# Rotary halves exchanged by transfers within SBUF in place of TensorE products, in a two-block transformer kernel on one core

## The chip, the cores and the metric

The kernel runs on one NeuronCore of one Trainium2 chip. The metric is the device time of one execution in microseconds (us), and of several executions the median. Engines are named as in the profile: PE is TensorE (PEld its weight loads), DVE is VectorE, ACT is ScalarE, POOL is GpSimd, SP is SyncE. A name with a q (ACTq, SPq) is that engine's queue where it issues a DMA.

## What is computed

Two transformer blocks run one after the other on 512 tokens of width 1024 (the second on 528, with 16 meta tokens in front). Only the first block's attention input matters here. The normalised input is projected to latent queries and keys and to the queries and keys of a dilated attention. Each head is normalised, and four kinds of head tile are then rotated by position:

```python
def rope(x, positions):
    d = x.shape[-1]
    half = d // 2
    inv_freq = jnp.power(ROPE_THETA, -2.0 * jnp.arange(half) / d)
    ang = positions[:, :, None, None] * inv_freq
    cos, sin = jnp.cos(ang), jnp.sin(ang)
    x1, x2 = x[..., :half], x[..., half:]
    return jnp.concatenate([x1 * cos - x2 * sin, x1 * sin + x2 * cos], axis=-1)
...
qd = rope(rms_norm(qd, g_dil_q), positions)          # 8 heads of 64
kd = rope(rms_norm(kd, g_dil_k), positions)          # 8 heads of 64
q_pe = rope(rms_norm(q[..., 64:], g_mla_q_pe), positions)   # 8 heads of 32
k_pe = rope(rms_norm(k_pe, g_mla_k_pe), positions)          # one of 32, shared by the heads
```

So each element needs itself times a cosine, plus its partner half a head away times a sine, with a minus sign in the first half. The attentions, the output projection, the two feed-forward stages and the second block (a state-space mixer and a gated recurrent mixer) follow and are not touched.

## The kernel before

Activations lie transposed: features on the 128 partitions, 512 tokens along the free axis. Weights come in units of 128 x 1024 float32 (512 KB) through two stage buffers, loaded by SP. ACT rounds each unit to a high part (`split_hi`, L906, instruction L912), and DVE forms the low part (`split_lo`, L2148, instruction L2151). PE multiplies three times per 128 x 128 block, high by high, high by low and low by high (`products`, L1458, instruction L1467). There are four slots of high and low parts, so ACT splits a unit only when the job that used its slot has ended (L911), and SP loads a stage buffer only when DVE has finished the unit in it (`stage_free`, L694).

Each engine's instructions stand in one order written out by hand, and semaphores join them. `Plan` only counts units and jobs. `ahead(name, j)` on ACT and on DVE (L993, L2333) splits the unit four ahead of the one that job `name, j` has just made free.

The stage around the change runs the jobs ql, kvl, dq (4 tiles), dk (4), qp (2), kpe (1), kn (4), qn01 (2) and qn23 (2), then the values mv and dv. A job is one tile of 128 features, 24 products for ql to dk and kpe, 12 for qp and qn, 6 for kn. Jobs alternate between two accumulators, so job n waits until ACT has read job n-2. ACT's `raw` (L1028) reads a finished job twice, once squared into `sqg` (L1043) and once times its gain into the tile's place in `HT` (L1048). The head tiles form five groups (`GROUPS`, L568): group 0 is dq, 1 is dk, 2 is qp and kpe, 3 is kn, 4 is qn. The first three are rotated, in six pieces (`ROTS`, L616): two pieces of two tiles for each group, but for the last, (2,1), which is the kpe tile alone.

For a group the four engines work as follows.

- PE's `group_stats` (L1673, L1682) sums the squares of a head with a block matrix of ones, once the squares are there, into PSUM banks 4 to 7.
- ACT's `group_log` (L1058, L1062) and `group_exp` (L1065, L1068) make the inverse root, each behind a load of its function table.
- PE's `group_rot` (L1685, instruction L1695) multiplies each tile of a piece by a signed permutation matrix `r64` or `r32` of the constants and so puts the partner half, with its sign, into PSUM banks 1 and 3. It waits for the tiles from ACT and for DVE to have read the banks for the piece before.
- POOL's `cosines` (L2992, L2997) multiplies the tiles in place in `HT` by the cosines, when PE's products are done.
- DVE's `rotated` (L2338) multiplies PSUM by the sines into `rtp` (L2345), waits for POOL, and adds `rtp` to `HT` (L2349). DVE's `scaled` (L2351, L2356) multiplies a whole group by the inverse roots and signals `ghead_done`.

`sqg` is two buffers that groups take in turn. So ACT's first `raw` of group g waits for `scaled` of group g-2 (L1042): kn 0 waits for group 1, and qn01 0 for group 2.

The tables of cosines and sines are made by DVE (`table`, L2202) from the positions and the inverse frequencies in the constants `misc`, and ACT takes the sine of all four at L1085.

The order on ACT from there is: raw dk 0, raw dk 1, group_log(0), raw dk 2, group_exp(0), raw dk 3, raw qp 0, ahead kpe, group_log(1), raw qp 1, group_exp(1), raw kpe, raw kn 0, raw kn 1, group_log(2), raw kn 2, group_exp(2), raw kn 3, raw qn01 0, group_log(3), and so on (L1086 to L1109). The order on DVE is at L2388 to L2415, that on PE at L1720 to L1745, and that on POOL at L3013 to L3021.

Transfers that ACT issues before are loads of parameters at the start (L976), stores of spilled tiles (L1260) and, in the state-space part, moves within SBUF (L1283). SP moves rows of `HT` within SBUF ahead of the second attention (L786 to L794).

## Time and profile before

| | us |
|---|---|
| median of 3 runs | 1760.17 |
| lowest and highest | 1756.51, 1763.28 |
| the profiled execution, its own time | 1757.67 |
| its span, first to last instruction | 1755.9 |
| PE busy in it | 1696.6 (97%) |

The profile shows one execution. Its span is 1.8 us shorter than the time of the same execution. Rows give starts in us from the span's start, then lengths in us, unless marked as nanoseconds. A matmul of float32 operands is recorded as two passes, so 11 products of PE stand as 22 in a row. A bracket at the end of a row gives the idle time of that engine ahead of the instruction and the instruction that ended it.

### The profile page before, as it was taken

Reading aid. Unit: us, or ns where it says so; the run is one execution under the profiler, and the core shown is the slowest. Engines: PE = TensorE matmul, PEld = TensorE weight load, DVE = VectorE, ACT = ScalarE, POOL = GpSimd, SP = SyncE. Lnnn points to the kernel's source line nnn. Section 1 sums busy time; section 2 is a strip of 40 time slices with the busy share of each in tenths; the row PEclk is TensorE's granted clock in tenths of the full one; section 3 lists DMA queues with packets and bytes.
Section 4 is the critical chain, followed back from the end, with each engine's and each line's share of the span. In section 5 each row is a group of like instructions: output and inputs, shape, how many; then the busy total and the mean of one; then the engine's idle time right before and its main releaser. Section 6 shows DMA issues by size and latency. Waiting matters only on the chain.

```text
span 1755.9 us, 32153 instructions
## 1 busy us (share of the span) xinstructions
PE 1696.6 (97%) x12653; PEld 1507.2 (86%) x12653; DVE 1091.8 (62%) x1748; ACT 744.7 (42%) x1111; POOL 298.1 (17%) x286
## 2 busy tenths in 40 slices
PE   5999999999999999899999999999999999999998
PEld 4776766788888888799999999999999899989986
DVE  6756577677664578855868663343753766654633
ACT  4367574465332342632323544346233643322323
POOL 2112196311000002532005221110102000000002
PEclk8999999999999999999999999999999999999999
DMA  9354532433333232263435752332543233332332
GB/s 311 110 145 106 157 109 74 143 89 104 96 96 108 84 98 73 80 180 119 131 104 159 218 138 86 97 109 81 167 120 97 65 92 96 89 102 84 96 94 75
DMA packets 321167, 201.17 MB, mean 115 GB/s; under 512 B 51280, under 2 KB 303815, under 8 KB 320919
## 3 DMA queue, kind: packets, MB, share of 16 engines
q1 hardware_dynamic: 300976, 160.79, 32.2%
q0 software_dynamic: 7952, 24.83, 4.7%
q10 hardware_dynamic: 12118, 13.88, 2.3%
q8 instruction: 84, 1.38, 0.3%
q14 instruction: 37, 0.30, 0.0%
HBM read 177.75 MB, written 17.24 MB: 111 GB/s over the span
## 4 chain that ended last, share of the span: by engine, by line
PE 82%; DVE 7%; ACT 4%; issue 2%; SPq 2%; DMA 1%; POOL 1%; ACTq 0%; DVEq 0%; POOLq 0%
PE ps L1467 68%; SPq L854 2%; DVE wlo L2151 1%; PE ps L1768 1%; PE ps L1667 1%; PE ps L1778 1%; PE ps L1794 1%; PE ps L1608 1%; PE ps L1998 1%; PE ps L1682 1%; DVE acol L2226 1%; PE ps L2094 1%; PE ps L1584 1%; ACT whi L912 1%; PE ps L2090 1%
## 5 line engine op out<-in xcount | busy, mean ns | idle before, releaser
L1467 PE MATMUL ps<-zhi,whi 128*128 128x258 f32 (+2 forms) x2072 | 638.5, 308 | 3.4 <-DVE wlo L2151 1.4
L1467 PE MATMUL ps<-zlo,whi 128*128 128x258 f32 (+2 forms) x2072 | 633.5, 306 | 0.0
L1467 PE MATMUL ps<-zhi,wlo 128*128 128x258 f32 (+2 forms) x2072 | 632.1, 305 | 0.0
L1467 PEld LDWEIGHTS ps<-zhi,whi 128*128 128x128 f32 x2072 | 390.9, 189 | 28.1 <-issue 3.0
L2151 DVE TENSOR_TENSOR wlo<-stage,whi 128x1024 fp32r<-128x1024 f32 x256 | 322.5, 1261 | 139.0 <-ACT whi L912 127.1
L1467 PEld LDWEIGHTS ps<-zlo,whi 128*128 128x128 f32 x2072 | 390.2, 188 | 19.3 <-issue 1.0
L1467 PEld LDWEIGHTS ps<-zhi,wlo 128*128 128x128 f32 x2072 | 390.9, 189 | 18.2
L912 ACT ACTIVATE whi<-stage 128x1024 fp32r<-128x1024 f32 x256 | 269.3, 1054 | 315.8 <-PE ps L1467 260.2
L1467 PE MATMUL ps<-ghi,whi 128*128 128x512 f32 x340 | 134.7, 396 | 0.0
L1467 PE MATMUL ps<-glo,whi 128*128 128x512 f32 x340 | 134.2, 395 | 0.0
L1467 PE MATMUL ps<-ghi,wlo 128*128 128x512 f32 x340 | 134.0, 394 | 0.0
L1201 ACT ACTIVATE ub<-ps 128x512 f32<-128x512 f32 (+1 forms) x88 | 52.6, 597 | 162.7 <-PE ps L1467 161.4
L3034 POOL TENSOR_TENSOR zu<-zu,sq 128x528 f32<-128x528 f32 (+1 forms) x18 | 31.7, 1760 | 425.5 <-ACT sq L920 424.6
L2564 DVE TENSOR_SCALAR cv<-ub,par 128x512 f32<-128x512 f32 (+1 forms) x88 | 49.0, 557 | 70.2 <-ACT ub L1201 70.2
L1211 ACT ACTIVATE ghi<-cv 128x512 f32 (+1 forms) x44 | 27.9, 634 | 124.5 <-DVE cv L2579 124.5
L1467 PEld LDWEIGHTS ps<-ghi,wlo 128*128 128x128 f32 x340 | 64.0, 188 | 15.0
L1467 PEld LDWEIGHTS ps<-ghi,whi 128*128 128x128 f32 x340 | 63.9, 188 | 14.7
L1467 PEld LDWEIGHTS ps<-glo,whi 128*128 128x128 f32 x340 | 63.9, 188 | 14.6
L3027 POOL TENSOR_SCALAR pb<-pb,small 128x128 f32<-128x128 f32 (+3 forms) x64 | 72.8, 1155 | 9.9 <-DVE small L2454 9.5
L2573 DVE SCALAR_TENSOR_TENSOR cv<-ub,par,cv 128x512 f32<-128x512 f32 (+1 forms) x88 | 66.3, 754 | 13.1 <-DVE cv L2567 6.7
L2480 DVE TENSOR_TENSOR xT<-ps,xT 128x512 f32 (+2 forms) x30 | 20.8, 692 | 85.1 <-PE ps L1467 85.1
L1258 ACT ACTIVATE spill<-ps 128x516 f32<-128x516 f32 (+1 forms) x40 | 24.1, 604 | 103.1 <-PE ps L1467 103.0
(426 smaller groups left out, 2854.4 us busy)
## 6 DMA issues: line engine op xcount, KB each, us to landing
stage<-in_w_up_dram SPq DMA_DIRECT2D x88, 512.0 KB, 3.8
stage<-in_w_in_dram SPq DMA_DIRECT2D x74, 512.0 KB, 4.0
stage<-in_w_down_dram SPq DMA_DIRECT2D x32, 512.0 KB, 3.9
ring<-in_w_ada_dram POOLq DMA_DIRECT2D x24, 512.0 KB, 4.6
adab<-in_w_ada_dram SPq DMA_DIRECT2D x16, 512.0 KB, 8.2
stage<-in_w_down_dram SPq DMA_DIRECT2D x16, 384.0 KB, 3.4
stage<-in_w_o_dram SPq DMA_DIRECT2D x8, 512.0 KB, 4.0
ring<-in_w_ada_dram SPq DMA_DIRECT2D x8, 512.0 KB, 3.8
```

The source lines that it names most:

```text
L854: sp.dma_start(y5[SH * g:SH * g + SH, k, :].rearrange("p (j c) -> p j c", j=LC), y_view[g])\
L912: act.activation(whi[u % NHL][:], stage[slot][:], ACT.Copy).then_inc(hi_done, 1)
L1201: act.activation(wide(ub[:, j % 2, 2:2 + T], T), acc(job, T), ACT.Copy).then_inc(emptied[job % 2], 1)
L1211: act.activation(ghi[c % 2][:, bass.ds(i * 2 + q, 1), 0:T].rearrange("p a t -> p (a t)"), cv[:, q, 1, 0:T], ACT.Copy).then_inc(ghi_done, 1)
L1258: act.activation(wide(spill[m % 2][:, T2 - T:T2], T), acc(n, T), fn).then_inc(emptied[n % 2], 1)
L1467: last = pe.matmul(out, w(a, k), x(k, t0, t1), start=(k == 0 and a is whi and x is x_hi), stop=(k == ks - 1 and a is wlo))
L2151: dve.tensor_tensor(wlo[u % NHL][:], stage[plan.w_load[u] % NST][:], whi[u % NHL][:].bitcast(F32), ALU.subtract).then_inc(split_done, 1)
L2480: ins = dve.tensor_tensor(x, acc(job, T), x, ALU.add)
L2564: link(dve.tensor_scalar(o, ub[:, g, 2:2 + T], tap(2), par[:, bass.ds(i * 2 + (ROW[f["cb"]] + ft), 1)], ALU.mult, ALU.add))
L2573: dve.scalar_tensor_tensor(out=o, in0=ub[:, g, 0:T], scalar=tap(0), in1=o, op0=ALU.mult, op1=ALU.add).then_inc(conv_done, 1)
L3027: pool.tensor_scalar(pb[:, t % 4, r, 0:w], pb[:, t % 4, r, 0:w], total(t, r, 32), None, ALU.mult)\
L3034: pool.tensor_tensor(square(n, 0), square(n, 0), square(n, 1 + j % 2), ALU.add).then_inc(acc_done, 1)
```

## The change

PE's products with the signed permutation are gone, with `rot` and the two matrices in the constants. ACT issues transfers from `HT` to `rtp` that exchange the halves, 4 for a piece of heads of 64 (each of 32 partitions) and 8 for a piece of heads of 32 (each of 16 partitions), 32 in all. The minus sign goes into the frequencies: those of the first half are negative, which leaves the cosine as it was and turns the sine's sign. DVE's product with the sines reads `rtp` in place of PSUM and is one instruction for two tiles. `gsin_done` is now signalled by DVE's final addition, so a piece's transfers, which write `rtp`, wait for the addition of the piece before.

```diff
@@ host_constants
-    misc[:, 0], misc[:, 1] = inv64, inv32
+    misc[:, 0], misc[:, 1] = np.where(p % 64 < 32, -inv64, inv64), np.where(p % 32 < 16, -inv32, inv32)
...
-    return np.concatenate([ident, ones, misc, b64, b32, rot(64), rot(32)] + mla + dil + [chunk],
+    return np.concatenate([ident, ones, misc, b64, b32] + mla + dil + [chunk],
...
+        TURN_DMAS = [P // (GROUPS[g]["w"] // 2) for g, _ in ROTS]
+        TURNS_IN = [16 * sum(TURN_DMAS[:i + 1]) for i in range(len(ROTS))]
+        JOB_OF = {t: job for job, (t, g, _) in RAW.items() if g >= 0}
@@ ACT
+            def half_turn(g, p):
+
+                t0, n, _ = piece(g, p)
+                i, h = ROTS.index((g, p)), GROUPS[g]["w"] // 2
+                for t in range(t0, t0 + n):
+                    wait_job_out(act, JOB_OF[t])
+                if i:
+                    act.wait_ge(gsin_done, i)
+                for r in range(0, P, 2 * h):
+                    for d, f in ((r, r + h), (r + h, r)):
+                        act.dma_start(rtp[d:d + h, 0:n, :], HT[f:f + h, t0:t0 + n, :]).then_inc(grot_in, 16)
...
             act.activation(tab[:, :, :], tab[:, :, :], ACT.Sin).then_inc(tab_done, 1)
+            half_turn(0, 0)
             raw("dk", 0)
             raw("dk", 1)
+            half_turn(0, 1)
             group_log(0)
             raw("dk", 2)
             group_exp(0)
             raw("dk", 3)
+            half_turn(1, 0)
             raw("qp", 0)
             ahead("kpe", 0)
             group_log(1)
+            half_turn(1, 1)
             raw("qp", 1)
             group_exp(1)
+            half_turn(2, 0)
             raw("kpe", 0, False)
             raw("kn", 0)
             raw("kn", 1)
+            half_turn(2, 1)
             group_log(2)
             raw("kn", 2)
             group_exp(2)
@@ PE
-            def group_rot(g, p):
-                t0, n, _ = piece(g, p)
...
-                for m in range(n):
-                    mm = pe.matmul(ps[:, 1 + 2 * m, :], const("r%d" % GROUPS[g]["w"]), HT[:, t0 + m, :], start=True, stop=True)
-                mm.then_inc(grot_mm, 1)
...
-            group_rot(0, 0)
...
-            group_rot(2, 1)
@@ DVE, rotated
-                dve.wait_ge(grot_mm, i + 1)
+                dve.wait_ge(grot_in, TURNS_IN[i])
                 dve.wait_ge(tab_done, 1)
-                for m in range(n):
-                    ins = dve.tensor_tensor(rtp[:, m, :], ps[:, 1 + 2 * m, :], tab[:, w + 1, :], ALU.mult)
-                ins.then_inc(gsin_done, 1)
+                link(dve.tensor_tensor(rtp[:, 0:n, :], rtp[:, 0:n, :], tab[:, w + 1:w + 2, :].to_broadcast([P, n, T1]),
+                                       ALU.mult))
+                dve.wait_ge(gcos_done, i + 1)
+                dve.tensor_tensor(HT[:, t0:t0 + n, :], HT[:, t0:t0 + n, :], rtp[:, 0:n, :], ALU.add).then_inc(gsin_done, 1)
                 dve.wait_ge(gsin_done, i + 1)
-                dve.wait_ge(gcos_done, i + 1)
-                link(dve.tensor_tensor(HT[:, t0:t0 + n, :], HT[:, t0:t0 + n, :], rtp[:, 0:n, :], ALU.add))
@@ POOL, cosines
-                pool.wait_ge(grot_mm, ROTS.index((g, p)) + 1)
+                pool.wait_ge(grot_in, TURNS_IN[ROTS.index((g, p))])
```

## Rows read from the trace of the kernel before

**Rows 1.** The page: engines' busy time, and shares of the chain that ended last

```profile
PE 1696.6 (97%) x12653; PEld 1507.2 (86%) x12653; DVE 1091.8 (62%) x1748; ACT 744.7 (42%) x1111; POOL 298.1 (17%) x286
PE 82%; DVE 7%; ACT 4%; issue 2%; SPq 2%; DMA 1%; POOL 1%; ACTq 0%; DVEq 0%; POOLq 0%
```

**Rows 2.** The chain that ended last, 60 to 230 us: start, length, what

```profile
112.43 1.72 PE ps L1695 x4
...
143.97 2.81 PE ps L1467 x12
...
153.58 1.92 ACT sqg L1068
...
163.68 1.10 PE ps L1695 x2
...
168.95 3.43 PE ps L1682 x8
172.39 2.79 PE ps L1467 x12
```

**Rows 3.** The line of PE's products with the permutation: ns min/median/max

```profile
L1695 PE MATMUL ps<-HT,cst x22: 590/592/667, 112.3 to 164.2; 128*128 128x512 f32 x22
```

**Rows 4.** Timeline of ACT, 130 to 164 us: start, length, line, operation

```profile
130.52 0.60 ACT L1043 ACTIVATE sqg<-ps 128x512 f32<-128x512 f32 x1 [4.39 <-PE ps L1467]
...
147.94 1.28 ACT L1062 ACT_TABLE_LOAD   x1
149.23 1.98 ACT L1062 ACTIVATE sqg<-ps,small 128x2048 f32<-128x2048 f32 x1
151.11 0.58 ACT L1043 ACTIVATE sqg<-ps 128x512 f32<-128x512 f32 x1
...
156.45 1.06 ACT L912 ACTIVATE whi<-stage 128x1024 fp32r<-128x1024 f32 x1
...
161.54 1.54 ACT L1062 ACTIVATE sqg<-ps,small 128x1536 f32<-128x1536 f32 x1
```

**Rows 5.** Loads of the qn weights by SP, 131 to 143 us: issues; KB each, landing

```profile
130.92 11.44 SPq L703 DMA_DIRECT2D stage<-in_w_q_b_dram  x14
stage<-in_w_q_b_dram SPq DMA_DIRECT2D x14, 64.0 KB, 2.1
```

**Rows 6.** Lines of the rotation on POOL and DVE: duration ns min/median/max

```profile
L2997 POOL TENSOR_TENSOR HT<-HT,tab x6: 1296/2484/2956, 114.8 to 164.9; 128x1024 f32<-128x1024 f32 x5, 128x512 f32<-128x512 f32 x1
L2349 DVE TENSOR_TENSOR HT<-HT,rtp x6: 693/1226/1226, 117.4 to 166.3; 128x1024 f32<-128x1024 f32 x5, 128x512 f32<-128x512 f32 x1
```

**Rows 7.** A DVE line with two SBUF inputs, alone and beside POOL's product

```profile
L2324 DVE SCALAR_TENSOR_TENSOR asum<-ring,csil,asum x14: 1277/1282/3391, 98.3 to 208.8; 128x1024 f32<-128x1024 f32 x14
157.24 2.88 POOL L2997 TENSOR_TENSOR HT<-HT,tab 128x1024 f32<-128x1024 f32 x1 [5.71 <-PE ps L1695]
157.81 3.39 DVE L2324 SCALAR_TENSOR_TENSOR asum<-ring,csil,asum 128x1024 f32<-128x1024 f32 x1
```

**Rows 8.** Issues and landings of transfers by line, ns and us

```profile
L1283 ACTq DMA_DIRECT2D TT<-K x32: 592/646/1497, 882.3 to 974.8; - x32
DMA to landing us min/median/max: 2.1/3.2/4.8
L791 SPq DMA_DIRECT2D HT<-HT x2: 603/656/708, 220.3 to 221.7; - x2
HT<-HT SPq DMA_DIRECT2D x2, 128.0 KB, 2.4
887.70 0.33 ACTq L1260 DMA_DIRECT2D f_scratch<-spill  x1
888.13 1.06 ACT L912 ACTIVATE whi<-stage 128x1024 fp32r<-128x1024 f32 x1 [0.46 <-ACT spill L1258]
```

**Rows 9.** Busy time and granted clock (PEclk) by stretch, us

```profile
15.60:25.85 10.25, 6.81 (x53) 5.61 (x52) 9.82 (x19) 6.19 (x10) 0.00 (x0) 0.98 0.94 278
25.85:36.10 10.25, 7.21 (x22) 5.82 (x23) 8.94 (x17) 3.64 (x6) 0.00 (x0) 0.52 1.02 337
```

More of the change, by code:

```diff
@@ L72, in host_constants @@
     b32 = (p[:, None] // 32 == p[None] // 32) * 1.0
-    def rot(w):
-        r = np.zeros((P, P))
-        for m in range(P):
-            j = m % w
-            if j < w // 2:
-                r[m + w // 2, m] = -1.0
-            else:
-                r[m - w // 2, m] = 1.0
-        return r
     qi, ki = p[:, None], p[None]
@@ L101, in host_constants @@
     misc[:, 64:] = p[:, None] // 16 == 2 * (p[None, :64] // 16)
-    return np.concatenate([ident, ones, misc, b64, b32, rot(64), rot(32)] + mla + dil + [chunk],
+    return np.concatenate([ident, ones, misc, b64, b32] + mla + dil + [chunk],
                           axis=1).astype(np.float32)
-CONST = {n: i * P for i, n in enumerate(["ident", "ones", "misc", "b64", "b32", "r64", "r32", "mla", "_m1",
+CONST = {n: i * P for i, n in enumerate(["ident", "ones", "misc", "b64", "b32", "mla", "_m1",
                                          "_m2", "_m3", "dil", "_d1", "_d2", "_d3", "chunk"])}
@@ L419, in emit @@
         lat_sum = sem("lat_sum")
-        grot_mm, gcos_done, gsin_done, ghead_done = (sem("grot_mm"), sem("gcos_done"),
+        grot_in, gcos_done, gsin_done, ghead_done = (sem("grot_in"), sem("gcos_done"),
                                                               sem("gsin_done"), sem("ghead_done"))
@@ L1683, in group_stats @@
                 mm.then_inc(gstat_mm, 1)
-            def group_rot(g, p):
-                t0, n, _ = piece(g, p)
-                last = [J["dq"] + 3, J["dk"] + 3, J["qp"] + 1][g] if (g, p) != (2, 1) else J["kpe"]
-                wait_job_out(pe, last)
-                wait_job_out(pe, last - 1)
-                if g == 0 and p == 0:
-                    pe.wait_ge(s_cst2, 16)
-                if (g, p) != (0, 0):
-                    pe.wait_ge(gsin_done, ROTS.index((g, p)))
-                for m in range(n):
-                    mm = pe.matmul(ps[:, 1 + 2 * m, :], const("r%d" % GROUPS[g]["w"]), HT[:, t0 + m, :], start=True, stop=True)
-                mm.then_inc(grot_mm, 1)
             lat = (zx(lhi), zx(llo))
@@ L1720, in _ @@
             z1("dk", 0)
-            group_rot(0, 0)
             z1("dk", 1)
             group_stats(0)
-            group_rot(0, 1)
             z1("dk", 2)
@@ L1728, in _ @@
             several("qp", 0, 4, lat)
-            group_rot(1, 0)
             group_stats(1)
             several("qp", 1, 4, lat)
-            group_rot(1, 1)
             z1("kpe", 0)
             several("kn", 0, 2, kvl)
-            group_rot(2, 0)
             several("kn", 1, 2, kvl)
```

## The prediction

> **What bounds the kernel now.** I read the page first: PE is busy 97% of the span and holds 82% of the chain that ended last [rows 1]. By that alone, any PE time removed would come off the total. The share is an average, so I then read the chain through the stage of the change, 104 to 215 us. The reader is to see three parts in it [rows 2]. Up to 146.8 us it is PE's products without a gap, the permutation among them. From the end of qp 1 (143.97 + 2.81 = 146.78) it lies on ACT and DVE: the split of a unit, group 1's logarithm and exponential, then `scaled`, one sum of DVE, a split and a product, until PE's last permutation product starts at 163.68 [rows 2, 7]. Then PE again, until qn01 1 ends at 172.39 + 2.79 = 175.18. So in the last third of the rotations ACT has no room [rows 4]: from 147.94 to 166 its rows follow each other almost without a gap.
>
> From 175.18 on, ACT, PE and DVE hand on to each other with no part of the change among them. I take it that a shift of that moment goes through to the end, since everything behind is bound by PE in order. So the question is where the end of qn01 1 goes.
>
> **What is removed.** 22 recorded passes of 0.59 us, overlapping [rows 3]: a pair of products takes 1.72 us of the chain, the single one 0.86 (half of it; its row reads 1.10, behind an idle of PE) [rows 2]. That is 5 x 1.72 + 0.86 = 9.5 us. Three pairs lie ahead of the end of qp 1, where PE bounds: 5.2 us come off, and qp 1 ends at 141.6. The other 4.3 us lie where ACT bounds, and count only as far as ACT lets them. PE's wait for the banks goes too, and two blocks of constants fewer are loaded; nobody waits for them, so nothing.
>
> **What is added on ACT.** 32 issues. An issue holds the queue: the store at 887.70 takes 0.33, and the next ACTIVATE starts at 888.13 [rows 8]. For a transfer within SBUF no row has exactly this shape. Nearest are ACT's own, 0.646 us at the median, and SP's of rows of the same tile, 0.603 and 0.708; a store to HBM at 0.33 is the low end, and 0.9, between the median and the longest row of 1.5, the high end for a mean over eight. I take 0.65: 2.6 us for a piece of four, 5.2 for one of eight, 4 x 2.6 + 2 x 5.2 = 20.8 us in all. From the last issue to landing I take 2.4, the 128 KB of the same tile; bounds 2.1 and 4.8 [rows 8].
>
> The Trainium skill, "DMA: Bandwidth & Descriptors", section on issuing engines not being separate DMA queues, says that the sequencer time of an issue is usually small beside the transfer. Taken at its word it would make this the second case below, not the sum: four issues at 2.6 us are no smaller than a landing of 2.4.
>
> **What is added on DVE and POOL.** The product with the sines becomes one instruction of 128 x 1024 with two SBUF inputs, 1.22 us like the addition [rows 6], where before it were two from PSUM. It is released together with POOL's cosines (2.4 us) by the same semaphore. Side by side they don't overlap: a DVE line of two SBUF inputs that takes 1.28 us alone took 3.39 when it started 0.57 us into POOL's product, and ended 1.08 after it (157.81 + 3.39 against 157.24 + 2.88) [rows 7]. So from landing to the end of the addition a piece takes 2.4 + 1.15 + 1.22 = 4.8 us; without the collision it would be 3.7.
>
> **Waits added.** ACT waits in `half_turn` for DVE's addition of the piece before, and behind that wait stand its raws, which free PE's accumulators. That is how the delay reaches PE.
>
> **The sum, walked in order.** The first three pieces are covered. (0,0) is issued at 111.5 to 114.1, its addition ends by 121; (0,1) is issued 121.6 to 124.2 and done by 130.9; (1,0) is issued 134.8 to 137.4, done by 145.2. ACT waited 4.39 us for PE in that stretch [rows 4], and raw dk 2, exp 0 and raw dk 3 still come about 2 us earlier than before. If that cover were gone, these three would cost up to 7.8 us more. SP's loads of qn23 hang on DVE's split of kn, behind `scaled` 0: its last issue was at 142.4 [rows 5], becomes about 140.2, and lands 2.1 later. ACT's split of qn23 therefore starts at about 142.4, not 146.9. POOL's ring loads keep their places.
>
> From there, with the lengths of [rows 4] (split 1.05, raw 1.1, logarithm of four 3.25 with its table, of three 2.8, exponential 3.2 [rows 2] and 2.8):
> - split to 143.4, log 1 to 146.65, issues of (1,1) to 149.25, raw qp 1 to 150.3, exp 1 to 153.5 (before: 155.5, still 2 ahead);
> - (1,1) lands at 151.0, addition done at 155.85. ACT stands 2.4 us before it may issue (2,0): 155.9 to 161.1, landing at 162.85;
> - raw kpe, split, raw kn 0, raw kn 1 to 165.4. DVE's split of the mv unit starts into POOL's cosines and ends at 166.4, then product and addition to 168.8. ACT stands 3.4 us, issues (2,1) to 174.0;
> - log 2 to 176.8, raw kn 2 to 177.9, exp 2 to 180.7, raw kn 3 to 181.8;
> - PE: sums of group 3 from 181.3 (3.43), qn01 1 to 187.55.
>
> Against 175.18 that is **+12.4 us**. In terms: 9.5 us of PE gained, of which 4.5 still stand at ACT's split, against 13.0 of issues behind it ((1,1), (2,0), (2,1)), 5.8 of waiting for DVE, less 1.9 of waits of before that are swallowed: -4.5 + 13.0 + 5.8 - 1.9 = 12.4. With both low ends (0.33 and 2.1) the same walk gives 180.9, +5.7; with both high ends (0.9 is then cut to 0.9 x 8 = 7.2 an octet, landing 4.8) 195.5, +20.3.
>
> The profiled execution took 1757.67 (span 1755.9 and 1.8 around it), 2.5 below the median of 1760.17; runs spread from 1756.5 to 1763.3. The shift is added to the median: 1772.6.
>
> **The rivals.**
> - *Issues cost nearly nothing, or overlap ACT's work.* With none at all, landing and collision as above, the walk gives qn01 1 at 176.9: +1.7, or 1762. It decides below about 0.2 us an issue. Against it: rows of ACT's queue at 0.65, with nothing beside them. For it: the store at 0.33, and that each new transfer has few, long rows. I put here everything between +1 and +6.
> - *Faster: PE's time comes off.* If besides cheap issues POOL and DVE did not collide, the waits for `gsin_done` shrink, and the walk gives 172.2: -3; with all 9.5 us realised, -9.5, or 1750.7. It needs issues under 0.1 us and landings that ACT never waits for. PE's 97% speaks for it; the ACT rows from 147 us speak against.
> - *PE's clock falls.* In my walk PE works only about 11 us of the 30 between 151.7 and 181. A stretch in which it was busy 6.8 of 10.25 us was followed by one at a clock of 0.52, half of 2.4 GHz [rows 9]. At half speed qn01 0 would end at 183.5, the sums of group 3 at 190.4 and qn01 1 at 196.0, 8.5 later: +20.9, or 1781. Against it: at half speed the work ahead would fill PE and might bring the clock back in time.
> - *The change doesn't do what it says.* The diff leaves no permutation product, so the PE time must go; the cosine is even, the sine odd. No chance of its own.
>
> **How the numbers follow.** 0.5% is 8.8 us, about what a measurement of this kernel tells from no change. The forecast, +7 to +18, has 0.52, of which 0.05 is below 8.8; the fallen clock 0.17; cheap issues 0.24; faster 0.07, of which 0.04 is beyond 0.5%. So slower 0.47 + 0.17 = 0.64, same 0.05 + 0.24 + 0.03 = 0.32, faster 0.04. The range runs from +1 (1761) to +24 (1784): it leaves out the faster case, 0.07, a fringe of cheap issues below +1, 0.06, and what a fallen clock together with long landings would give beyond, 0.06.
>
> **What the profile after would show.** Right: no L1695; ACTq rows of 0.6 us in fours and eights, ACT's next row only behind them; an idle of 2 to 4 us of ACT ahead of (2,0) and (2,1), ended by DVE's addition; that sine product at well over 1.22 us, or POOL's cosines at over 2.4, in most pieces; qn 1 of qn01 ending near 187.5; PE with gaps of some 10 us between 150 and 180. Wrong: ACT's ACTIVATEs running beside the issues, issues near 0.3, landings under 2, or qn01 1 ending before 175.2. Wrong in size: a granted clock of a half in 160 to 190, or issues over 0.8 while SP is issuing too. If qn01 1 ends 12 us late and the total is not longer, then the assumption that the shift goes through was the error.

## The result and the profile after

The changed kernel takes **1780.1 us** (median of 4 runs, 1777.1 to 1781.9) against 1760.0 beside it: ratio **1.0117 (95% interval 1.0103 to 1.0130)**, slower by 20.1 us. The forecast was 1772.6, slower, with a range of 1761 to 1784. So the sign and the range held, and the sum of +12.4 was 7.7 us short. Where those are is the main question below.

The profiled execution has a span of 1777.3, against 1755.9. Two moments cut that difference of 21.4 into three parts. The first is the start of ACT's sine of the tables, just ahead of the first product of the rotation (L1085 before, L1090 after). The second is the start of `raw` qn01 1, from where on the prediction let the shift go through.

| | before | after | difference |
|---|---|---|---|
| start to sine | 109.63 | 111.79 | +2.2 |
| **stage**: sine to raw qn01 1 | 65.57 | 80.53 | +15.0 |
| **rear**: raw qn01 1 to the end | 1580.7 | 1585.0 | +4.3 |

The profiles are single executions. That of the kernel before took 1757.7, 2.5 below the median of 1760.2; that of the changed kernel took 1779.2, 0.9 below its median. If start and stage grew in every execution as in these two, the medians leave 20.1 - 2.2 - 15.0 = 2.9 us for the rear (an estimate), not 4.3.

First the page's busy time and shares of the chain, which answer to [rows 1].

```profile
PE 1697.6 (96%) x12631; PEld 1510.9 (85%) x12631; DVE 1095.6 (62%) x1743; ACT 744.8 (42%) x1111; POOL 298.7 (17%) x286
PE 79%; DVE 6%; ACT 4%; issue 3%; SPq 2%; DMA 2%; POOL 2%; ACTq 1%; DVEq 0%; POOLq 0%
```

PE made 22 passes fewer and was still busy 1.0 us longer, since part of its work ran at a lower clock (last view of this section). Its share of the chain went from 82% to 79%.

The timeline of ACT, 147 to 178 us, answers to [rows 4]: start, length, engine, line, operation, and in brackets the idle time ahead and what ended it. L1053 is the new transfer, L1036 and L1041 are `raw`.

```profile
147.51 1.06 ACT L905 ACTIVATE whi<-stage 128x1024 fp32r<-128x1024 f32 x1 [2.39 <-DMA stage<-in_w_q_b_dram]
148.18 0.51 ACTq L1053 DMA_DIRECT2D rtp<-HT  x1
148.59 1.28 ACT L1067 ACT_TABLE_LOAD   x1
148.72 1.26 ACTq L1053 DMA_DIRECT2D rtp<-HT  x2
149.89 1.97 ACT L1067 ACTIVATE sqg<-ps,small 128x2048 f32<-128x2048 f32 x1
150.01 0.61 ACTq L1053 DMA_DIRECT2D rtp<-HT  x1
...
154.23 1.91 ACT L1073 ACTIVATE sqg<-sqg 128x2048 f32<-128x2048 f32 x1
159.50 5.00 ACTq L1053 DMA_DIRECT2D rtp<-HT  x8
164.55 0.60 ACT L1036 ACTIVATE sqg<-ps 128x512 f32<-128x512 f32 x1 [8.41 <-issue]
...
168.81 0.60 ACT L1036 ACTIVATE sqg<-ps 128x512 f32<-128x512 f32 x1 [1.07 <-PE ps L1478]
169.30 0.68 ACT L1041 ACTIVATE HT<-ps,par 128x512 f32<-128x512 f32 x1
172.45 5.00 ACTq L1053 DMA_DIRECT2D rtp<-HT  x8
177.48 1.28 ACT L1067 ACT_TABLE_LOAD   x1 [7.50 <-issue]
```

The four issues of (1,1) stand beside a split, a table load and the logarithm, and cost ACT nothing. The octets of (2,0) and (2,1) stand alone: ACT idles 8.41 and 7.50 us, of which 5.0 each are issues, the rest (3.4 and 2.5) a wait for the piece before. These two idles, 15.9 us, are about as long as the whole growth of the stage, 15.0.

What ACT waits for is in the timelines of DVE and POOL (L2336 product with the sines, L2339 addition, L2347 `scaled`, L2143 split, L2988 cosines). They answer to [rows 6, 7].

```profile
130.66 1.22 DVE L2336 TENSOR_TENSOR rtp<-rtp,tab 128x1024 f32<-128x1024 f32 x1 [5.80 <-DMA rtp<-HT]
134.25 1.23 DVE L2339 TENSOR_TENSOR HT<-HT,rtp 128x1024 f32<-128x1024 f32 x1 [2.37 <-POOL HT L2988]
135.51 1.23 DVE L2143 TENSOR_TENSOR wlo<-stage,whi 128x1024 fp32r<-128x1024 f32 x1
...
154.65 1.23 DVE L2336 TENSOR_TENSOR rtp<-rtp,tab 128x1024 f32<-128x1024 f32 x1 [4.74 <-DMA rtp<-HT]
158.17 1.22 DVE L2339 TENSOR_TENSOR HT<-HT,rtp 128x1024 f32<-128x1024 f32 x1 [2.30 <-POOL HT L2988]
```

```profile
118.62 2.53 POOL L2988 TENSOR_TENSOR HT<-HT,tab 128x1024 f32<-128x1024 f32 x1
130.70 3.44 POOL L2988 TENSOR_TENSOR HT<-HT,tab 128x1024 f32<-128x1024 f32 x1 [9.55 <-DMA rtp<-HT]
154.69 3.38 POOL L2988 TENSOR_TENSOR HT<-HT,tab 128x1024 f32<-128x1024 f32 x1 [10.11 <-DMA rtp<-HT]
```

The last issue of (1,1) starts at 150.01 and its data land 4.6 us later, where DVE takes them up at 154.65, not 2.4. Then DVE's product (start 154.65) and POOL's (154.69) collide. DVE is 0.04 us ahead and takes its usual 1.23; POOL takes 3.38, and the addition waits 2.30 for it. (2,0) is issued when that addition ends. The Trainium skill, "SBUF — State Buffer", section on who interferes with whom, says that a DVE instruction with two SBUF inputs contends with a GpSimd instruction that reads SBUF, that the ports they share are an exclusive lock, and that the order of issue decides who blocks. The trace agrees in both directions: where POOL was ahead, at 118.62, DVE's product took 3.40.

Last PE's busy time and granted clock by stretch; they answer to [rows 9]. A row has the stretch and its length, the busy time and number of instructions of PE, PEld, DVE, ACT and POOL, then the granted clock as a share of 2.4 GHz, the DMA share and GB/s.

```profile
147.00:154.00 7.00, 5.00 (x22) 3.80 (x21) 2.30 (x2) 6.44 (x6) 0.00 (x0) 1.00 0.94 226
154.00:160.00 6.00, 1.07 (x4) 0.31 (x2) 3.02 (x3) 2.13 (x2) 3.38 (x1) 0.51 0.00 0
160.00:171.00 11.00, 5.13 (x9) 3.18 (x10) 7.18 (x5) 4.36 (x7) 2.37 (x1) 0.50 0.32 51
171.00:182.00 11.00, 4.88 (x17) 3.19 (x16) 3.57 (x3) 4.49 (x5) 1.80 (x2) 0.81 0.30 79
182.00:188.00 6.00, 6.00 (x17) 3.97 (x16) 3.35 (x3) 5.63 (x8) 0.00 (x0) 0.76 0.18 70
```

PE was busy 1.07 us of the 6 from 154 on, and from there to 171 it got half of 2.4 GHz. It idled again (6.12 us ahead of 181.53) and the clock was 0.76 on average in the last stretch, where its work stands on the chain.

### The profile page after: what moved, and what is told of

Read it like the earlier page. It is cut to its first block, busy times and chain, and to the rows that moved or that the text cites. A ratio compares the mean times of both kernels' runs of the same rounds, so it can differ in the third digit from the quotient of the medians.

```text
span 1777.3 us, 32136 instructions
## 1 busy us (share of the span) xinstructions
PE 1697.6 (96%) x12631; PEld 1510.9 (85%) x12631; DVE 1095.6 (62%) x1743; ACT 744.8 (42%) x1111; POOL 298.7 (17%) x286
## 4 chain that ended last, share of the span: by engine, by line
PE 79%; DVE 6%; ACT 4%; issue 3%; SPq 2%; DMA 2%; POOL 2%; ACTq 1%; DVEq 0%; POOLq 0%
PE ps L1478 65%; SPq L847 2%; PE ps L1595 1%; DVE wlo L2143 1%; PE ps L1619 1%; PE ps L1760 1%; PE ps L1678 1%; PE ps L1770 1%; PE ps L1786 1%; PE ps L1990 1%; ACT whi L905 1%; PE ps L2086 1%; POOL HT L2988 1%; DMA xrow<-in_x_dram 1%; PE ps L2082 1%
## 5 line engine op out<-in xcount | busy, mean ns | idle before, releaser
L2143 DVE TENSOR_TENSOR wlo<-stage,whi 128x1024 fp32r<-128x1024 f32 x256 | 325.2, 1272 | 139.8 <-ACT whi L905 127.7
L3025 POOL TENSOR_TENSOR zu<-zu,sq 128x528 f32<-128x528 f32 (+1 forms) x18 | 31.6, 1757 | 425.6 <-ACT sq L913 424.7
L3018 POOL TENSOR_SCALAR pb<-pb,small 128x128 f32<-128x128 f32 (+3 forms) x64 | 72.7, 1154 | 9.6 <-DVE small L2445 9.2
```

Of the source, the lines that this page charges most:

```text
L2143: dve.tensor_tensor(wlo[u % NHL][:], stage[plan.w_load[u] % NST][:], whi[u % NHL][:].bitcast(F32), ALU.subtract).then_inc(split_done, 1)
L3018: pool.tensor_scalar(pb[:, t % 4, r, 0:w], pb[:, t % 4, r, 0:w], total(t, r, 32), None, ALU.mult)\
L3025: pool.tensor_tensor(square(n, 0), square(n, 0), square(n, 1 + j % 2), ALU.add).then_inc(acc_done, 1)
```

## The experiments

Stage and rear are cut as above. Medians are of the runs named by the experiment, ratios against the kernel before on the same chip, with 95% intervals.

| | what | us | ratio | stage | rear |
|---|---|---|---|---|---|
| before | | 1760.2 | | 65.6 | 1580.7 |
| after | | 1780.1 | 1.0117 (1.0103 to 1.0130) | 80.5 | 1585.0 |
| e1 | after, again | 1779.2, one run | | 80.6 | 1585.0 |
| e2 | two buffers | 1767.9 | 1.0047 (1.0033 to 1.0061) | 69.4 | 1587.7 |
| e3 | one transfer a piece | 1764.3 | 1.0022 (1.0010 to 1.0033) | 66.5 | 1587.2 |
| e4 | cosines apart | 1768.3 | 1.0051 (1.0035 to 1.0066) | 72.8 | 1582.3 |
| e5 | before, products cut | 1755.7 | 0.9977 (0.9968 to 0.9987) | 61.7 | 1579.9 |
| e6 | POOL issues | 1788.9 | 1.0163 (1.0149 to 1.0177) | 86.4 | 1588.4 |
| e7 | e2 and e4 | 1765.7 | 1.0035 (1.0022 to 1.0049) | 68.7 | 1582.7 |
| e8 | three pieces by PE | 1759.2 | 1.0000 (0.9990 to 1.0011) | 65.1 | 1580.0 |
| e9 | before, +17.2 on PE | 1777.6 | 1.0101 (1.0087 to 1.0116) | 82.7 | 1580.8 |
| e10 | before, +6.9 on PE | 1767.3 | 1.0044 (1.0031 to 1.0057) | 72.7 | 1581.8 |
| e11 | e8, splits first | 1765.4 | 1.0031 (1.0019 to 1.0043) | 69.9 | 1585.3 |
| e12 | e8 without a stall | 1759.0 | 0.9989 (0.9979 to 0.9999) | 62.4 | 1584.7 |

### e1: the changed kernel a second time

> The changed kernel as it is, for a second profile. In its first profile the end of qn01 1 came 17.1 us later than before (192.3 against 175.2), of which 2.0 us were there at 95 us, ahead of every part of the change, and the end came 21.4 us later, 4.3 us more, with three short stretches of half clock behind 320 us that the profile before doesn't have. Theory: the rotary stage itself costs 15 us, and the 2.0 and the 4.3 belong to the execution; a second profile then shows another split of them, with the stage (from the sine at L1090 to the end of qn01 1, 80.5 us in the first) within 1.5 us of the first. Rival: they belong to the change, and come back at the same places within 0.3 us.

Stage 80.6, rear 1585.0, each within 0.1 us of the first profile, and the sine starts at 111.79 again. The rival held: the parts repeat. But both executions took 1779.2 us, so they say little about the slower ones, up to 1781.9, and nothing about the kernel before.

### e2: two buffers for the swapped halves

```diff
-        rtp = at("rtp", [P, 2, T1], TAB + 8192 + 4096)
+        rtp = [at("rtp0", [P, 2, T1], TAB + 8192 + 4096), at("rtp1", [P, 2, T1], SQO)]
...
-                if i:
-                    act.wait_ge(gsin_done, i)
+                if i > 1:
+                    act.wait_ge(gsin_done, i - 1)
...
```

> Transfers go to two buffers in turn, so ACT waits for DVE's addition of the piece before the last, not of the last. Theory, that ACT stands for DVE's addition ahead of both pieces of eight (3.4 us and 2.5 us in the profile, and the issues could start earlier still, beside the exponential): 8 us less than the changed kernel, a ratio of about 1.007 to the kernel before, and raw kpe some 6 us earlier. Rival, that what costs is the time of the eight issues alone (5.0 us twice): at most 2 us less, ratio 1.010 or more. Rival, the fallen clock: no change of the ratio beyond 0.001.

The total fell by 12 us and the stage by 11.2, more than the 8 expected. ACT's timeline shows why one wait is worth more than its own length:

```profile
149.10 1.28 ACT L1074 ACT_TABLE_LOAD   x1
149.16 1.80 ACTq L1054 DMA_DIRECT2D rtp<-HT  x3
150.39 1.91 ACT L1074 ACTIVATE sqg<-sqg 128x2048 f32<-128x2048 f32 x1
150.98 3.17 ACTq L1054 DMA_DIRECT2D rtp<-HT  x5
154.20 0.60 ACT L1037 ACTIVATE sqg<-ps 128x512 f32<-128x512 f32 x1 [1.89 <-issue]
```

Without the wait, (2,0)'s octet runs beside the table load and the exponential, so ACT idles 1.89 us where it idled 8.41. The wait was not only 3.35 us long: it also parted the issues from the work that hid them.

### e3: one transfer for a piece

```diff
-                for r in range(0, P, 2 * h):
-                    for d, f in ((r, r + h), (r + h, r)):
-                        act.dma_start(rtp[d:d + h, 0:n, :], HT[f:f + h, t0:t0 + n, :]).then_inc(grot_in, 16)
+                act.dma_start(rtp[:, 0:n, :], HT[:, t0:t0 + n, :]).then_inc(grot_in, 16)
```

> One transfer of 128 partitions in place of the 4 or 8 of a piece: the same bytes and waits, 6 issues in place of 32. It leaves out the exchange of the halves. Theory of issues on the path: the pieces of eight hold ACT 0.4 us instead of 5.0; half of that is given back, since the bytes of a piece land about 4.8 us behind one issue where they landed 2.2 behind the last of eight: about 6 us less than the changed kernel, ratio 1.008. Rival, the bytes and their landing are the cost: no more than 2 us less, ratio 1.010 or more. If all 9.2 us come off, landing was off the path, ratio 1.006.

It leaves out the exchange of the halves. Six issues of 0.47 us in place of 32 of 0.61 bring the stage to 66.5, 14.1 less and 0.9 from the kernel before, and the total falls by 15.8. I had expected 6, or 9.2 if landing was off the path, so the theory had the direction and less than half of the size: besides the issues of the octets, each piece starts and lands earlier (ACT's split of qn01 starts 27.3 us behind the sine, not 31.2), and DVE's splits and the weights with it. The waits for additions are still there (1.77 us, and 3.75 ahead of group 2's logarithm), but each starts earlier. The edit changes the shape of a transfer together with the number of issues, and the run does not part the two.

### e4: cosines into a buffer of their own

```diff
-                pool.wait_ge(grot_in, TURNS_IN[ROTS.index((g, p))])
...
+                for t in range(t0, t0 + n):
+                    wait_job_out(pool, JOB_OF[t])
...
-                pool.tensor_tensor(HT[:, t0:t0 + n, :], HT[:, t0:t0 + n, :],
+                pool.tensor_tensor(cosb[:, 0:n, :], HT[:, t0:t0 + n, :],
...
+            pool.wait_ge(gsin_done, len(ROTS))
```

> POOL writes the products with the cosines to a buffer of their own, while the transfer is in flight, and DVE adds both into HT. POOL is then done before the transfer lands: from landing to the end of the addition a piece takes 2.5 us where it took 4.8, since POOL and DVE no longer collide or wait. Theory, collision and POOL's product lie on the path in (1,1) and (2,0): 4.5 us less than the changed kernel, ratio 1.009. Rival, they are hidden behind ACT's issues: no change, ratio within 0.001 of 1.0117.

POOL no longer starts with DVE at the landing. The stage falls by 7.8 and ACT's idles ahead of the two octets' next rows become 4.49 and 5.97 us. The total falls by 11.8, where 4.5 were expected; the 4.0 beside the stage are start and rear. The collision, with POOL's product behind it, was a real term: in the stage it is worth less than the buffer (7.8 against 11.2), in the medians the two can't be told apart (1768.3 and 1767.9).

### e5: PE's products cut from 512 columns to 4

```diff
-  mm = pe.matmul(ps[:, 1 + 2 * m, :], const("r%d" % GROUPS[g]["w"]), HT[:, t0 + m, :], start=True, stop=True)
+  mm = pe.matmul(ps[:, 1 + 2 * m, 0:4], const("r%d" % GROUPS[g]["w"]), HT[:, t0 + m, 0:4], start=True, stop=True)
```

> The kernel before, with each permutation product of PE cut from 512 columns to 4. Left out: the partner's half for all but 4 tokens, so most of the sine part of the rotation. Everything waits for the same things as before, only PE's time of these products is gone. This prices what the change removes. Theory (the prediction's): of the 9.5 us on PE, 5.2 come off where PE bounds (three pairs ahead of the end of qp 1) and the rest lies where ACT bounds, so about -5 us, 1755, a ratio of 0.997. Rival, by PE's share of 97%: all of it, -9.5 us, 0.9946. Rival, late stretches at half clock fall otherwise when the program is shifted: up to 4 us more or less than the shift of qn01's last square.

-4.7 us between the medians, -3.9 in the stage: the theory held. This is the whole prize of the change: less than half of the 9.5 us that PE spends on these products. So the transfers, with what hangs on them, cost the stage 80.5 - 61.7 = 18.8 us.

### e6: POOL issues the transfers

```diff
+                        pool.dma_start(rtp[d:d + h, 0:n, :], HT[f:f + h, t0:t0 + n, :]).then_inc(grot_in, 16)
...
             def cosines(g, p):
+                half_turn(g, p)
...
-            half_turn(2, 0)
             raw("kpe", 0, False)
```

> The changed kernel, but POOL issues the transfers, right in front of its cosines, and ACT issues none and waits for no addition. Same transfers, same landings, same collision of POOL with DVE. Theory: what the stage lost is ACT standing and issuing in front of group 2; with both gone from ACT, about 12 us of the 20 go, as with two buffers or cosines made early: 1768, a ratio of 1.0045. Between 1764 and 1768 if the 10 us of octets issued by ACT alone come off as well and POOL has room. Rival: landings and additions set the time whoever issues them, and POOL's issues, in front of its own product, move them later: 1776 to 1782, near the changed kernel.

The theory fell: 8.8 us slower than the changed kernel, with an ACT that issues nothing, and slower than the rival's 1776 to 1782 too. POOL's timeline shows each piece as one closed ring: issue, landing, product, addition, next issue.

```profile
116.91 0.53 POOL L684 DMA_DIRECT2D ring<-in_w_ada_dram  x1 [2.84 <-DVE asum L2298]
117.45 1.97 POOL L2975 DMA_DIRECT2D rtp<-HT  x4
125.56 3.43 POOL L2983 TENSOR_TENSOR HT<-HT,tab 128x1024 f32<-128x1024 f32 x1 [6.14 <-DMA rtp<-HT]
...
161.21 2.15 POOL L2975 DMA_DIRECT2D rtp<-HT  x4 [1.91 <-DVE HT L2321]
168.53 3.37 POOL L2983 TENSOR_TENSOR HT<-HT,tab 128x1024 f32<-128x1024 f32 x1 [5.17 <-DMA rtp<-HT]
173.82 3.91 POOL L2975 DMA_DIRECT2D rtp<-HT  x8 [1.91 <-DVE HT L2321]
```

From one issue to the next are 12.6 us (161.21 to 173.82), and group 1's `scaled`, for which ACT then waits 8.65 us with raw kn 0, hangs on it. The issues also got a later place: the first starts at 117.45, behind a load of `ring`, where ACT's started at 109.37. So this run is bounded by the closed ring through one buffer, and taking ACT out of it does not help. Together with e2, where a second buffer opens the ring and takes 11.2 us off the stage, it says that the changed kernel is bounded by that ring too, with ACT's octet issues as a part of it. For the changed kernel this is argued from the two runs, not measured by itself.

### e7: two buffers and the cosines apart

> The changed kernel with both repairs at once: two buffers for the swapped halves, and the cosines into a buffer of their own, made as soon as the tiles are there. ACT issues. Theory: each alone took off some 12 us by taking the same wait away (ACT standing for DVE's addition), so together they give little more: 1764 to 1767, 1.003 to 1.004; what is left are the issues, 10 us of octets, of which about half is covered. Rival: the two add, 1757 or below, 0.998. Rival: late landings of the first four pieces, which hold up DVE's splits and so qn23's weights, are the floor, 1768 as each alone.

The edits of e2 and e4 together. 1765.7, stage 68.7: the first theory held. ACT still idles 1.90 and 4.28 us for issues, and its splits of qn01 and qn23 still wait for loads (3.43 and 2.22 us).

### e8: three pieces by transfers, three by PE

```diff
+            def group_rot(g, p):
...
+                i = ROTS.index((g, p))
+                if i < NTURN:
+                    return
...
+                if i:
+                    pe.wait_ge(gsin_done, i)
+                for m in range(n):
+                    mm = pe.matmul(ps[:, 1 + 2 * m, :], const("r%d" % GROUPS[g]["w"]), HT[:, t0 + m, :], start=True, stop=True)
...
```

`NTURN` is 3.

> A mix: the first three pieces by transfers of ACT, as in the changed kernel, the last three by PE's products, with an unsigned permutation, as before. It keeps the gain where PE bounds, 5.2 us of products, and leaves the pieces where ACT bounds to PE. Theory: -3 us against the kernel before, 1757, 0.998. Rival: the three covered pieces already cost as much as they give, since each lands 4 to 5 us after its last issue and DVE's splits wait behind that: 0 to +3, 1.000 to 1.002. Rival: all of the loss is behind the third piece but the start is later by 0.6 to 2.2 us in each kernel with these transfers: 0.9995.

Ratio 1.0000, stage 0.5 shorter than before: the theory fell, and the first rival held. PE idled 4.25 us before the first of its products, until 147.96, for DVE's addition of (1,0). That addition stood behind DVE's split of a unit whose load SP had issued late. So the three pieces that ACT covers look to be paid for by DVE's splits and the weights; e11 and e12 try that.

### e9 and e10: the kernel before with more sums on PE

```diff
-                for m in range(len(s["tiles"])):
+                for m in list(range(len(s["tiles"]))) * (6 if g == 3 else 1):
```

> The kernel before, in which PE forms group 3's sums of squares six times in place of once (same operands, same banks, same results), between qn01 0 and qn01 1. One time takes 3.43 us, so this moves everything from qn01 1 on by 17.2 us with PE busy in it: a shift nearly as long as that of the changed kernel, with no transfer, no wait of ACT and no idle of PE. It asks whether a shift goes through to the end. Theory: not one to one. Where the program's gaps of PE fall, the chip grants half the clock for a few us or doesn't, and that differs with the shift: the stage gives 17.2, the rest of the program -1 to +7 beside its 1580.7 of the kernel before, so 1776 to 1784. Rival: it goes through exactly, 1777.3, and the rear of the changed kernel is 4 us longer for a reason in its own instructions.

> The same with three times in place of once: 6.9 us of shift. Rival (exactly through): 1767.0. Theory: 6.9 and -1 to +7 of the rest, with stretches at half clock at other places than with five more; two shifts whose totals do not lie on one line with the kernel before would show it.

In e10 the 6 is a 3. The stage grew by 17.2 and 7.1, the medians by 17.9 and 7.5 (against 1759.73 beside them), the rears by 0.1 and 1.1. The theory's ranges were wide enough to hold both, but the totals of 1777.6 and 1767.3 lie within 0.3 us of the rival's 1777.3 and 1767.0, and nothing asks for more: **a shift of this moment goes through to the end one to one**, as the prediction took it. Then the rear of the changed kernel's profile has 4.3 us that no shift explains. Since e9's raw qn01 1 starts at 192.77 and the changed kernel's at 192.32, the same stretches of both can be laid side by side. Busy time and granted clock of two stretches (the third, 745 to 753 us, reads 0.79 against 1.00 as well), first the changed kernel, then e9:

```profile
311.00:319.00 8.00, 5.71 (x32) 4.41 (x31) 3.27 (x4) 1.88 (x3) 0.60 (x1) 0.79 0.17 51
...
1048.00:1056.00 8.00, 5.61 (x41) 5.38 (x41) 4.62 (x10) 6.03 (x7) 1.23 (x1) 0.79 0.72 216
```

```profile
311.00:319.00 8.00, 5.70 (x38) 4.41 (x37) 3.27 (x4) 2.14 (x3) 0.72 (x2) 1.00 0.11 33
...
1048.00:1056.00 8.00, 7.10 (x67) 6.73 (x66) 5.77 (x12) 5.07 (x7) 0.63 (x1) 1.00 0.80 243
```

The same work, in the same places; the changed kernel has part of each stretch at the lower clock, and in the first makes 32 passes where e9 makes 38. PE's row of sums behind the first stretch (`ps<-cst,asum`) stands 135.23 us behind raw qn01 1 in the changed kernel, and 133.84 in e9 and in the kernel before: 1.4 us for that one. But row by row this loss does not stay the same. ACT's splits and the read of the gated unit (`ko`) at the third stretch, first the changed kernel, then e9, then the kernel before:

```profile
1042.51 1.06 ACT L905 ACTIVATE whi<-stage 128x1024 fp32r<-128x1024 f32 x1 [3.51 <-DMA stage<-in_w_in_dram]
1048.22 1.06 ACT L905 ACTIVATE whi<-stage 128x1024 fp32r<-128x1024 f32 x1 [4.65 <-DMA stage<-in_w_in_dram]
...
1060.77 0.60 ACT L1384 ACTIVATE ko<-ps 128x512 f32<-128x512 f32 x1 [4.88 <-PE ps L2030]
```

```profile
1043.18 1.06 ACT L912 ACTIVATE whi<-stage 128x1024 fp32r<-128x1024 f32 x1 [3.87 <-DMA stage<-in_w_in_dram]
1047.04 1.06 ACT L912 ACTIVATE whi<-stage 128x1024 fp32r<-128x1024 f32 x1 [2.80 <-DMA stage<-in_w_in_dram]
...
1058.01 0.60 ACT L1373 ACTIVATE ko<-ps 128x512 f32<-128x512 f32 x1 [3.33 <-PE ps L2038]
```

```profile
1023.87 1.06 ACT L912 ACTIVATE whi<-stage 128x1024 fp32r<-128x1024 f32 x1 [3.15 <-DMA stage<-in_w_in_dram]
1029.28 1.06 ACT L912 ACTIVATE whi<-stage 128x1024 fp32r<-128x1024 f32 x1 [4.35 <-DMA stage<-in_w_in_dram]
...
1040.25 0.60 ACT L1373 ACTIVATE ko<-ps 128x512 f32<-128x512 f32 x1 [2.17 <-PE ps L2038]
```

All counted from raw qn01 1. At the first of the rows the changed kernel is 1.5 us behind the kernel before, and 0.2 ahead of e9. To the second it loses 0.3 more against the kernel before; e9 gains 1.5 there, by an earlier landing of weights (the two rows are 3.9 us apart in e9, 5.4 in the kernel before, 5.7 in the changed kernel and 5.1 in its second profile, e1). From the second row to the third are 12.55 us in the changed kernel and 10.97 in the two others: 1.6 us. That distance goes by the mean clock between the two rows in all fourteen profiles: 12.5 to 12.6 us at 0.86 (the changed kernel, e1, e7, e11, e12), 13.6 to 13.9 at 0.75 (e2, e3, e6), and 10.96 to 10.98 at 1.00 (the others). So **of the 4.3 us, 1.6 are shown to be the clock's**. Of the rest, 1.5 have gathered ahead of the first row, 0.3 come between the first and the second, and 0.9 lie behind ACT's last row.

One thing limits what this says of other executions. e9's profiled execution was its fastest, 1775.4 us at a mean clock of 0.994; its other three took 1777.2 to 1778.9 at 0.991. 0.003 of 1776 us are 5.3 us of clock (an estimate), as much as three stretches of 8 us at 0.79 cost (5.0). The runs of the kernel before lie at 0.990 to 0.995 likewise. So such stretches may well come in other executions of both, which left no profile. Nor do they need the transfers: e5 has none, and its profile reads 0.79 in the second stretch, as e8's does. e4 has the first two, e7 only the third, e2 and e3 the first and the third.

### e11: the splits first

```diff
-            rotated(0, 1)
             ahead("dk", 2)
+            rotated(0, 1)
...
-            rotated(1, 0)
             ahead("kpe", 0)
+            rotated(1, 0)
```

> The mix with three pieces by PE, but DVE splits the unit that comes behind a piece of transfers before it takes up that piece (kpe's neighbour ahead of (0,1), kpe's ahead of (1,0)), so that SP's loads of qn01 and qn23 are not held up by a late landing. In the mix DVE's split stood at 135.26, behind an addition at 134.00 that had waited for the landing at 130.4; it would stand at 130.4, and the weights come up to 5 us earlier, which is where ACT waited for a transfer before the split at 142.82. Theory: 3 to 4 us less than the mix, 1755.5, a ratio of 0.9975. Rival: the weights are not what bounds, PE waits for ACT at group 1 in any case, no change from the mix: 1759, 1.000.

Both fell: 6 us slower than e8 in the medians. (The twelve runs lie from 1759.2 to 1770.0, two of them below 1760; the profiled one took 1768.1.) The loads did come early (SP's issues at 131.21, not 136.51), but the second swap put the addition of (1,0) behind a split that waits for them, and PE's product of (1,1) waits for that addition. PE, 130 to 163 us:

```profile
150.88 3.75 PE L1715 MATMUL ps<-HT,cst 128*128 128x512 f32 x4 [7.56 <-DVE HT L2377]
153.64 1.42 PE L1487 MATMUL ps<-zhi,whi 128*128 128x512 f32 x1
154.86 0.63 PE L1487 MATMUL ps<-zlo,whi 128*128 128x512 f32 x1
```

In the idle of 7.56 us and behind it the clock was at half: 0.50 from 147 to 152 and 0.52 from there to 157, and a product of 0.39 us is recorded as 0.63.

### e12: the mix without that stall

```diff
-                if i:
+                if i > NTURN:
                     pe.wait_ge(gsin_done, i)
...
```

> The mix with three pieces by PE, and two edits: PE's first product of the rotation, for piece (1,1), no longer waits for DVE's addition of (1,0), whose data went through a transfer and used no PSUM bank; and DVE splits the unit behind (0,1) before it takes up (0,1) (the second swap of the run with the splits first is not made: there the addition of (1,0) stood behind a split at 147.11, PE idled 7.56 us for it and was at half clock from 146.7 to 156.9). In the mix PE idled 4.25 us for that addition, until 147.96, and again 1.16 and 1.31 us of ACT were waits for PE behind it. Theory: this idle was what ate the 5.2 us of products; with it gone ACT bounds again, from the landing of qn's weights at about 145, and the time is 2 to 4 us below the mix, 1755 to 1757, a ratio of 0.997 to 0.9985. Rival: ACT's splits, which wait for those weights in both, bound by themselves: 1759, 1.000.

With this and only the first swap of e11, PE's idle ahead of (1,1) is gone, the products start at 141.67, and the stage is 62.4: 3.2 less than before, within 0.7 of e5, where the products are cut altogether. So what the theory said of the stage came true. The total did not: 1759.0 is the rival's number, not 1755 to 1757, and the ratio of 0.9989 lies between the two. The median is 2.2 us below the kernel before, with an interval that just excludes no change: a gain of 0.1%, not one to build on. The profile's rear is 4.0 us longer than before, with the clock at 0.79 in the same three places behind raw qn01 1 as in the changed kernel, each 20.0 us earlier. By the medians less is left for it: the change of -2.2 holds -3.2 of the stage and +0.3 of the start, which leaves +0.7 us (an estimate). Most of the 4.0 would then be the fast execution of the kernel before that was profiled.

## Why the prediction was right, and where its sum was short

The prediction's case happened: ACT stands for DVE's additions and issues the octets alone, so PE starts qn01 late. Of the 20.1 us the sum had 12.4. By its own steps, in the profile after less the 2.2 us by which the stage started later:

| step | predicted | after, less 2.2 |
|---|---|---|
| split of qn23 starts | 142.4 | 145.4 |
| exp 1 ends | 153.5 | 154.0 |
| addition of (1,1) ends | 155.85 | 157.2 |
| octet (2,0) issued | 161.1 | 162.3 |
| raw kn 1 ends | 165.4 | 167.8 |
| octet (2,1) issued | 174.0 | 175.3 |
| raw kn 3 ends | 181.8 | 183.1 |
| qn01 1 ends | 187.55 | 190.1 |

- **What is removed: right.** 9.5 us of PE, of which e5 realises 3.9 in the stage. The prediction had 5.2 ahead of qp 1 and the rest only as far as ACT lets it.
- **An issue at 0.65: right** (0.61 at the median, 5.0 for eight, not 5.2). **That every issue holds ACT: wrong.** The 2.6 us for (1,1) cost nothing, since they ran beside ACT's other rows, which the prediction had named as a sign of being wrong. An issue held back what stands behind it in the program, and not what stands ahead of it. [rows 8] were read as a queue that does one thing at a time.
- **Landing at 2.4 for a piece of four: wrong** for three of the four, 5.9, 5.2, 3.0 and 4.6 us from the start of the last issue. The octets landed as the prediction had it, in 2.3 (of 64 KB each) and 2.0 (32 KB). For (1,1), the one that counts, the bound of 4.8 in [rows 8] was nearer. These two errors nearly cancel, 2.6 less and 2.2 more, and that is luck: it is why the addition of (1,1) comes within 1.4 us of the walk.
- **qn23's weights at 142.4: wrong**, 3 us late: 1.5 earlier than before, not 4.5. The walk let DVE gain 2 us and had missed that DVE's split, which frees SP's load, stands behind `rotated`, and so behind a landing: 130.66, 134.25, 135.51 in the rows above. SP began the loads at 136.8 (130.0 before).
- **Collision: right.** An addition waits 2.3 us for POOL in both pieces shown. The prediction had DVE as the one that is stretched. That was so at (0,0) (3.40) and at (2,1) (1.80 for half the width, where 0.69 is usual); at (0,1) and (1,1), where DVE began 0.04 us ahead, it was POOL. At (2,0) DVE's split was stretched to 2.98, as the walk said. e4 puts the collision at 7.8 us of stage, with all that follows.
- **ACT's waits: right in sum, not in the parts.** Ahead of (2,0) ACT waited 3.4 us, not 2.4, since (1,1) landed late. Ahead of (2,1) it waited 2.5, not 3.4, since by then ACT itself was later, by the octet before and 1.07 us of waiting for PE. That 5.8 comes out as 5.8 is luck.
- **A fallen clock: the rival had part of it.** The half clock came from 154 on, as it said, and again behind 182. A clock of a half in 160 to 190 is the other sign of being wrong in size that the trace shows. It cost less than its 8.5: raw kn 1 waited 1.07 for PE, and from raw kn 3 to the end of qn01 1 are 7.1 us, not the 5.75 of the walk.
- **The shift goes through: right** (e9: 17.2 and 17.9). **That nothing is added behind: wrong.** The rear is 4.3 us longer in the profiles, some 3 by the medians. The term was put at nothing, on the ground that everything behind is bound by PE in order; 1.6 of it stand in one place 856 to 868 us behind, by a clock at half, and the rest is not traced to a cause. I know no view of the profile before that would have shown it.

In sum: of 21.4 us in the profile the walk had 12.4. The stage's other 2.6 are late weights, landing and clock, less the covered issues; 4.3 are the rear, and 2.2 the start. By the medians the 7.7 us that the sum lacked are about 2.6 of stage, 2.9 of rear and 2.2 of start. Of the 2.2 of the start, 1.7 are there at ACT's first read into `sqg` (65.97 against 64.29), long before the first transfer, and their cause is open. The other 0.5 go with the clock: from 76 to 86 us it reads 0.83 in the seven profiles in which the sine starts 45.8 to 46.0 us behind that read (the changed kernel, e1, e6, e7, e8, e10, e11), and 1.00 in the seven in which it starts 45.2 to 45.5 behind. e10 has no transfers, so this too is not theirs. In all, the sine starts between 109.45 and 110.96 in the four kernels without transfers, and between 109.54 and 112.46 in the others, which doesn't part them.

The rival of cheap issues is out for this kernel, though its reason was true for (1,1). One issue of 0.61 us is short beside its landing of 2.3; eight in a row took 5.0, and they stand in the ring through the one buffer (landing, product, addition, next issue) that bounds group 2. What the Trainium skill says in "DMA: Bandwidth & Descriptors", section on issuing engines not being separate DMA queues, that the time of an issue is usually small beside the transfer, does not hold for such an octet as a whole. e3 shows what the rival would have brought: with six issues in place of 32 the total was 4.1 above the kernel before (1764.3), inside the +1 to +6 that the rival gave.

**Open.** What decides in which executions the rear's half-clock stretches come was not settled. They repeat in the same program (e1) and are at the same three distances behind raw qn01 1 in the changed kernel, e11 and e12, but each was seen in one or two executions, and e9's mean clocks speak for it that they differ from one execution to the next. Why (1,1) takes 4.6 us to land was not tried apart. The shape alone isn't it, since (1,0) landed in 3.0, and (1,1) itself in 2.9 in e4. In the changed kernel weights were loaded beside it, at a DMA share of 0.94 in 147 to 154 us; in e4 the share was 0.64 from 146 to 149.

## What to carry to other kernels

Before work is moved from a bound engine to a queue, look at which instruction stands behind the wait that the move adds, and on which engine: here one buffer's reuse was worth 11 to 12 us, the number of issues 14 to 16 (the two overlap and don't add), and the PE time saved was worth 4. Here a transfer's issues were free beside queued work, and cost their full length behind a wait. Then follow what the late data hold up on the other engines, up to the loads of weights.

## What was not expected of the hardware

- ACT's transfers are issued while its ACTIVATEs and table loads run: 148.18 to 150.62 beside a split, a table load and a logarithm. Those of (0,0) even start at 109.37, ahead of the sine (111.79) behind which they stand in the program. They cost ACT time where the rows ahead of them had run out: 1.48 us at (0,1), 5.0 at each octet.
- POOL's issues are shorter than ACT's (0.49 against 0.61 us at the median for the same transfers), but their data came no sooner: 2.5 us to landing at the median and 6.6 at most, against 2.3 and 5.9.
- In the rear, 120 to 860 us behind the change, unchanged work ran at half clock in three short places. One cost 1.4 us at once, of which later rows keep a varying part; the last cost 1.6 us, the same in five profiles to within 0.1.
- Such stretches come and go between programs whose code there is the same, and they are not bound to transfers: one ahead of the stage (0.83 from 76 to 86 us) is in e10 and not in the kernel before.
